# Modulation of a two-layer trunk: split fp32r products in two blocks, or plain fp32 products spread between the stages, with the loads of x on another queue

## The reference, cut to what matters

```python
def ada_params(cond, w_mod, b_mod):
    m = jax.nn.silu(cond) @ w_mod + b_mod          # w_mod: 1024 x 6144, one per layer
    return jnp.split(m, 6, axis=-1)

for layer in range(2):
    mp, ms = ada_params(c_ctx, ...), ada_params(c, ...)
    h = rms_norm(x, norm1) * (1 + m[1]) + m[0]
    x = x + m[2] * mixer(h)                        # layer 0: even mixer (scan), layer 1: attention and convolution
    h = rms_norm(x, norm2) * (1 + m[4]) + m[3]
    x = x + m[5] * ff(h)                           # layer 0: dense SwiGLU, layer 1: mixture of 8 experts
```

## Time and profile before

| what | value |
|---|---|
| median of 3 runs | 2351.88 us (2350.11 to 2356.47) |
| the profiled execution | 2351.2 us, span 2349.6 us |
| PE, DVE, ACT, POOL busy | 84%, 54%, 36%, 14% |
| modulation of layer 0, PE | 31.0 to 105.2 us, with the turning of x in it |
| modulation of layer 1, PE | 867.3 to 933.8 us |
| last remainder of norm 0, of norm 2 | 153.0 us, 985.4 us |

### The profile page before, as it was taken

The page is one execution under the profiler, slowest core; times in us unless marked ns, Lnnn a source line. Parts: engine busy times, 40 slices in busy tenths (PEclk is TensorE's granted clock), DMA queues, the critical chain, the costliest instruction groups (busy, mean ns, idle before and its releaser), DMA issues.

```text
span 2349.6 us, 35825 instructions
## 1 busy us (share of the span) xinstructions
PE 1967.4 (84%) x12234; PEld 1730.1 (74%) x12235; DVE 1257.9 (54%) x2029; ACT 856.9 (36%) x1348; POOL 327.8 (14%) x350
## 2 busy tenths in 40 slices
PE   4789486999999996898878886697978888896985
PEld 2489285999999983795333574697967888896983
DVE  4733764223323347315987547244866777865435
ACT  4722712222122237222223322243644655553321
POOL 2030202000000000205960003002101011101011
PEclk9979787999999999698577897798989998998996
DMA  9902011324621249222000021246867699866433
GB/s 286 313 21 73 18 37 45 108 78 128 161 80 42 74 143 329 76 72 54 3 0 0 1 78 63 65 119 184 231 178 213 181 254 260 237 191 169 122 90 134
DMA packets 439521, 288.47 MB, mean 123 GB/s; under 512 B 20890, under 2 KB 428666, under 8 KB 439332
## 3 DMA queue, kind: packets, MB, share of 16 engines
q1 hardware_dynamic: 425124, 248.75, 36.6%
q0 software_dynamic: 13024, 37.12, 5.3%
q10 hardware_dynamic: 1184, 0.51, 0.1%
HBM read 262.86 MB, written 23.47 MB: 122 GB/s over the span
## 4 chain that ended last, share of the span: by engine, by line
PE 67%; DVE 15%; issue 9%; ACT 3%; SPq 2%; DMA 2%; POOL 1%; ACTq 1%; DVEq 0%; POOLq 0%
PE ps L983 14%; PE ps L984 14%; PE ps L985 14%; PE ps L988 11%; PE ps L989 4%; DVE vp L1824 2%; PE ps L1051 2%; SPq L464 2%; DVE lo L1555 2%; PE ps L1269 1%; PE ps L1286 1%; ACT hi L613 1%; POOL tmp L2208 1%; DVE am L1885 1%; DVE h_both L1646 1%
## 5 line engine op out<-in xcount | busy, mean ns | idle before, releaser
L1555 DVE TENSOR_TENSOR lo<-raw,hi 128x1024 fp32r<-128x1024 f32 (+3 forms) x538 | 566.6, 1081 | 200.6 <-ACT hi L613 195.7
L613 ACT ACTIVATE hi<-raw 128x1024 fp32r<-128x1024 f32 (+3 forms) x538 | 495.6, 942 | 403.5 <-PE ps L985 255.9
L983 PE MATMUL ps<-h_both,hi 128*128 128x320 f32 x1728 | 546.8, 316 | 62.4 <-DVE h_both L1646 30.4
L984 PE MATMUL ps<-h_both,hi 128*128 128x320 f32 x1728 | 541.7, 313 | 0.0
L985 PE MATMUL ps<-h_both,lo 128*128 128x320 f32 x1728 | 541.6, 313 | 0.0
L983 PEld LDWEIGHTS ps<-h_both,hi 128*128 128x128 f32 x1728 | 330.8, 191 | 72.7 <-issue 41.0
L988 PE MATMUL ps<-h_both,hi 128*128 128x256 f32 (+2 forms) x1056 | 295.6, 367 | 60.8 <-issue 52.0
L984 PEld LDWEIGHTS ps<-h_both,hi 128*128 128x128 f32 x1728 | 331.6, 192 | 0.2 <-issue 0.2
L985 PEld LDWEIGHTS ps<-h_both,lo 128*128 128x128 f32 x1728 | 331.2, 192 | 0.0
L988 PEld LDWEIGHTS ps<-h_both,hi 128*128 128x128 f32 x1056 | 211.7, 200 | 70.3 <-issue 53.2
L989 PE MATMUL ps<-h_both,lo 128*128 128x128 f32 (+2 forms) x1056 | 257.6, 244 | 0.0
(11 more groups left out here) (324 smaller groups left out, 2617.3 us busy)
## 6 DMA issues: line engine op xcount, KB each, us to landing
raw<-in_moe_w_dram SPq DMA_DIRECT2D x160, 512.0 KB, 5.2
raw<-in_w_mod_dram SPq DMA_DIRECT2D x96, 512.0 KB, 7.7
raw<-in_moe_w_dram SPq DMA_DIRECT2D x64, 384.0 KB, 3.5
raw<-in_ff_w_dram SPq DMA_DIRECT2D x40, 512.0 KB, 4.9
raw<-in_moe_w_dram SPq DMA_DIRECT2D x64, 320.0 KB, 3.8
y_rows<-zeros POOLq DMA_DIRECT2D x22, 512.0 KB, 4.2
raw<-in_moe_w_dram SPq DMA_DIRECT2D x32, 256.0 KB, 2.9
raw<-in_ev_w_in_dram SPq DMA_DIRECT2D x12, 512.0 KB, 8.8
```

The source lines that it names most:

```text
L613: act.activation(hi[c % 2][:, parts[h]], raw[c % 4][:, parts[h]], ACT.Copy).then_inc(hi_done, 1)
L983: pe.matmul(out, w_hi, v_hi, start=first, stop=False, skip_group_check=True)
L984: pe.matmul(out, w_hi, v_lo, start=False, stop=False, skip_group_check=True)
L1555: dve.tensor_tensor(lo[c % 2][:, parts[h]], raw[c % 4][:, parts[h]], hi[c % 2][:, parts[h]].bitcast(F32), ALU.subtract).then_inc(lo_done, 1)
```

## The change

The products of the modulation are made without a split. The stationary operand is `cs`, two columns of plain fp32, and the 256 moving columns come straight from the `raw` buffer, in plain fp32: 8 matmuls a chunk, and no `hi`, no `lo`. PE itself releases the buffer (`mod_done`). ACT copies the result to one of two short rows (`mod_row`), PE turns it at once with two transposes of 2 rows (`fold`), and where a group of chunks ends ACT copies the group out of PSUM (`mod_keep`) and DVE adds the bias (`mod_params`).

The 48 chunks no longer stand in two blocks. They come as 8 ahead of `EIN` (around the turning of x and around norm 0), 12 in the mixer, 8 behind the sums of norm 1, 8 around norm 2, 8 ahead of attention, 4 behind the sums of norm 3. The ring of buffers counts them in that order, so loads of the other weights move with them. `split` of the two chunks of the next projection now stands inside norm 0 and behind norm 3; it stood in the modulation's loop and behind `OOUT`. PE waits for `mod_kept` ahead of `EIN`, `EOUT`, `FF`, `OIN` (twice), the first product with v in attention, and the turning behind the router.

The loads of x are begun on ACT's queue right behind `mats`, ahead of the 21 loads of parameter rows; POOL's queue loses them and the load of `sel4`. The loops over the two `FF` items are written out on SP, ACT and DVE. The gates use six banks instead of eight and the swap one bank instead of two, so that the modulation has banks of its own.

```diff
+MODS = [(0, 8, 0), (8, 12, EOUT + 2), (20, 8, FF + 2), (28, 8, OIN + 2), (36, 8, OOUT + 2), (44, 4, MOE)]
+KEPT = [(0, 8), (8, 12), (20, 4), (24, 4), (28, 4), (32, 4), (36, 8), (44, 4)]
...
             act.dma_start(mats[:, :, :], a["const_mats"].rearrange("m p c -> p m c")).then_inc(mats_in, 16)
+            for t in range(TT):
+                src = a["x_prompt"][0] if t == 0 else a["x_sample"][0, (t - 1) * P:t * P, :]
+                act.dma_start(xrows[:, t, :], src).then_inc(x_in, 16)
             act.wait_ge(prow_zero, 1)
...
+            def mod_row(first, count=1):
+                for q in range(first, first + count):
+                    act.wait_ge(mod_done, q + 1)
+                    if q >= 2:
+                        act.wait_ge(mod_folded, q - 1)
+                    act.activation(mrow[:, q % 2, :], ps[0:2, mod_bank(q), 0:256], ACT.Copy).then_inc(mod_rows, 1)
...
-            mod_fours(0, X_AFTER)
+            mod_row(0, 4)
...
-            mod_fours(X_AFTER, N_MOD // 4)
+            mod_row(4, 2)
...
+                if first is not None:
+                    first()
                 for k in range(KT):
                     act.wait_ge(n_aff, KT * i + k + 1)
                     act.activation(hh[:, k, :], tmp[:, k % 2, 0:T] if h is None else h[:, k, :], ACT.Copy).then_inc(n_hi, 1)
+                    if with_k is not None and k % 2:
+                        with_k(k // 2)
...
+            def first_weights():
+                mod_row(6, 2)
+                mod_keep(0)
+                split_hi(EIN)
+                split_hi(EIN + 1)
...
+            norm_act(1, lambda k: (evac, 2 * (EOUT + k // 2 + 1)), first=lambda: mod_row(20), with_k=lambda c: mod_row(21 + c))
...
-            act.wait_ge(evac, 2 * M1)
-            mod_fours(0, N_MOD // 4 - 1, M1, mrow1)
...
+            norm_act(2, lambda k: (evac, 2 * OIN), first=rest_of_first, with_k=lambda c: mod_row(32 + c))
...
+            def mod_chunk(q):
+
+                r = ring_of_mod(q)
+                w = raw[r % 4][:, :].rearrange("p (k c) -> p k c", k=KT)
                 for k in range(KT):
...
+                    if k % (KT // 2) == 0:
+                        pe.wait_ge(slot_in[r % 4][k // (KT // 2)], 16 * landed(r))
+                    if k == 0 and q >= 2:
+                        pe.wait_ge(mod_rows, q if mod_bank(q) == 7 else q - 1)
+                    last = pe.matmul(ps[0:2, mod_bank(q), 0:256], cs[:, k, :], w[:, k, :], start=k == 0, stop=k == KT - 1, skip_group_check=True)
+                last.then_inc(mod_done, 1)
...
-            norm_pe(0)
-            fold(mrow)
+            mods(4, 2)
+            norm_pe(0)
+            mods(6, 2, True)
+            pe.wait_ge(mod_kept, 1)
...
+            mods(20, 8, True)
+            pe.wait_ge(mod_kept, 4)
...
-            with pe.Fori(0, N_MOD // 2) as pr:
-                for u in range(2):
-                    begin(M1 + 2 * pr + u)
-                    mod_chunk(u, M1 + 2 * pr + u)
+            mods(28, 2)
             pe.wait_ge(evac, 2 * OIN)
             norm_pe(2)
-            fold(mrow1)
+            mods(30, 2, True)
+            pe.wait_ge(mod_kept, 5)
+            mods(32, 4, True)
+            pe.wait_ge(mod_kept, 6)
```

More of the change, by code:

```diff
@@ L49, with ring_of, ring_of_mod, landed @@
 N_ITEM = N_UP + KT
[L50 to L57, removed]
+EIN, EOUT, FF, OIN, OOUT, MOE = 0, 6, 10, 50, 57, 61
+MODS = [(0, 8, 0), (8, 12, EOUT + 2), (20, 8, FF + 2), (28, 8, OIN + 2), (36, 8, OOUT + 2), (44, 4, MOE)]
+KEPT = [(0, 8), (8, 12), (20, 4), (24, 4), (28, 4), (32, 4), (36, 8), (44, 4)]
+X_BANKS = (4, 6, 7)
+def ring_of(n):
+    return n + sum(count for _, count, before in MODS if before <= n)
+def ring_of_mod(q):
+    return q + [before for first, _, before in MODS if first <= q][-1]
+MANY = [(ring_of(OIN + c), 3) for c in range(2)] + [(ring_of(OOUT + c), 1) for c in range(4)]
+def landed(r):
+    return r // 4 + 1 + sum(more for m, more in MANY if m <= r and m % 4 == r % 4)
+def taken_before(r):
+    for q in range(2 * N_MOD):
+        if ring_of_mod(q) == r - 4:
+            return "mod", q
+    for n in range(MOE):
+        if ring_of(n) == r - 4:
+            return "weight", n
 JH = 6
@@ L525, in _ @@
-            sp.dma_start(hsel[:, :, :], a["const_hsel"]).then_inc(odd_in, 16)
-            sp.dma_start(hspread[:, :, :], a["const_hspread"]).then_inc(odd_in, 16)
+                return up_proj, up_part, down_proj
+            mods(0)
+            for c in range(6):
+                load(EIN + c, columns(a["ev_w_in"][0], c * 256))
+            for c in range(2):
+                load(EOUT + c, columns(a["ev_w_out"][0], c * 256))
+            mods(1)
+            for c in range(2, 4):
+                load(EOUT + c, columns(a["ev_w_out"][0], c * 256))
@@ L626, in mod_fours @@
-            def mod_fours(start, end, first=M0, mrow=mrow):
-                with act.Fori(start, end) as pr:
-                    for u in range(4):
-                        mod_evac(u % 2, first + 4 * pr + u, 4 * pr + u, mrow)
-                        split_hi(first + u + 2, pr, fine=True)
-            mod_fours(0, X_AFTER)
+            act.activation(cs[:, :, 0], par[:, 1, CX:CX + KT], ACT.Silu)
+            act.activation(cs[:, :, 1], par[:, 1, CS:CS + KT], ACT.Silu).then_inc(cs_silu, 1)
+            act.wait_ge(ab_lam, 1)
@@ L993, in begin @@
                 pe.wait_ge(lo_done, 2 * n + 1)
[L994 removed]
+                if not isinstance(n, int) or n >= 2:
+                    pe.wait_ge(evac, 2 * (n - 1) if free is None else free)
             def second(n):
@@ L1641, in norm_dve @@
                 t_of(1)
+                if first is not None:
+                    first()
                 for k in range(KT):
-                    if k == 3 and layer is not None:
-                        mod_params(layer, 1)
                     dve.wait_ge(n_hi, KT * i + k + 1)
@@ L1648, in norm_dve, with first_weights @@
                         t_of(k + 2)
-            norm_dve(0, layer=0)
+            def first_weights():
+                mod_params(0, part=0)
+                split_lo(EIN)
+                split_lo(EIN + 1)
+            norm_dve(0, first=first_weights)
             for c in range(2):
```

382 lines of the change are left out of this document (205 added, 177 removed).

## The result

| | before | changed |
|---|---|---|
| median of the runs | 2350.99 us (4 runs, 2347.61 to 2356.47) | 2261.07 us (4 runs, 2253.32 to 2263.03) |
| profiled execution, its span | 2351.2 us, 2349.6 us | 2261.82 us, 2260.2 us |
| granted clock, mean | 0.892 | 0.926 |

The ratio is 0.9609, 95% interval 0.958 to 0.9639.

The account below looks back on a forecast made before the run. PE, busy 84% of the span, was taken to wait in stretches, among them both modulation blocks (DMA full, DVE nearly). Terms -48 + 6 + 10 - 67 + 16 + 6 = -77 on 2351.2 us gave 2274 us, range 2246 to 2312.

Parts of the forecast that it names:

- The price of a chunk: All 48 chunks on PE: 16 records, 3.55 us each at full clock, 3.9 with the two transposes.
- The first rival: Spread chunks don't raise the clock, 7.0 us each: 2320 in part (chance 0.15), 2440 throughout (0.03), no change (0.01).
- The start: Up to the last remainder of norm 0: at 104.9 us instead of 152.99, 48 us less.
- The second rival: At the start, parameter rows get nothing until x is through and land 13.5 us later, at 40: 2286 us; chance 0.12.
- The mixer: Mixer and `EOUT`: 12 chunks, 47 us, into 41 us of idle PE, clock gain gives back 3: 6 us more.
- Norm 1: From the sums to the feed-forward part's first products: eight chunks come first, 412.4 against 402.5, 10 us more.
- row 24 is copied behind k = 7, then chunks 26 and 27: End of norm 1: 402.7 + 0.4 + 3.9 + 3.9 + 1.5 = 412.4 us on the old time axis.
- Norm 2 and `OIN`: From the end of `FF`: 118 us to the last remainder before, now a sum of 51: 67 us less.
- ahead of attention: Between `OIN` and attention: five chunks at 1.5 us, two at 7.8 less 4, then 4: 16 us more.
- The third rival: Mixer and attention take their chunks for nothing, clock gains pay: 2252 us; chance of better than 2255: 0.13.
- Router: Four chunks behind the sums of norm 3, gated by norm copies; 1.5 less for splits before squares: 6 us more.
- Behind the router: From the end of the router's product to the end of the kernel: no difference, 0.

Follow-up runs that it names:

- the two blocks: Changed kernel with its plain fp32 chunks put back in two blocks of 24, ahead of `EIN` and behind the feed-forward part: 2364.08 us, ratio 1.0044.
- the kernel with standing weights: Changed kernel with the roles in a chunk's product exchanged: fp32 weights stand, two columns of silu(c) move, no row copies or transposes back: 2354.9 us, ratio 1.0043.

## Why the prediction was right

**The price of a chunk** came from the sums of norm 1, scaled by columns: 3.55 us, measured 3.6. With the fold 3.76 instead of 3.9, since the two transposes of 2 columns need 0.15 to 0.2 us in the sequence, not the 0.35 of two full ones. 48 x 0.14 is 7 us of PE's time, of which some 30% lie on the path: 2 us, spread over the stages below.

**The clock.** The first rival (low clock) needed records 0.43 us apart. They are 0.216 apart from 35.6 us on, but for two chunks: number 37 ahead of attention took 5.30 us behind a wait of 2.69 us, and number 46 ahead of the router 5.15 us behind one of 3.89. At the start the clock rose 5.6 us behind the first chunk, where I had taken 5. In norm 1 and the mixer the granted clock is 1.00.

**The start**, -48 against -48.5. The rows were due at 28.2 and came at 28.1, but the reason that I gave for it is only half of what happens. I had x begun at 11 us, as on GpSimd's queue. On ScalarE's it is begun from 1.47 us on, which pushes the issue of the last row from about 13 to 18.9 us; and that row lands 9.0 us after its issue instead of 13.5. The changed kernel's chain of waits has:

```profile
18.93 9.04 DMA prow<-in_k_norm_dram
```

5.8 later and 4.4 quicker is the 1.4 us measured. That the two nearly cancel to the forecast's 1.6 is luck. The second rival (rows that wait for x, 2286 us) put 13.5 us on the rows, from a landing of x that began at 11 us among the modulation's weights; begun at 1.47, x had landed at 22.8 us, and the last row at 28.0. The Trainium skill's "DMA: Bandwidth & Descriptors", section "Queues, rings and completion order", which stands behind it (a ring's descriptors are taken in order), isn't contradicted: the last row did land behind x, but x needed only 3.9 us more when that row was issued. The kernel with x on GpSimd's queue puts the price of being behind x at 2.0 us.

**The mixer**, +6 against +3.1. The mixer itself grew by 6.3 us, as forecast, though the clock rose in the whole stage (0.73 to 1.00). What I had not counted is `EOUT`: from its first product to the one from which it runs without a gap it took 7.75 us instead of 10.33, and 0.6 less from there on.

**Norm 1**, +10 against +12.9. The step "row 24 is copied behind k = 7, then chunks 26 and 27" is met: 9.8 us forecast from that copy's end to the first product, 358.69 to 368.51 measured. What was missing is clock, twice. The sums took 10.24 us instead of 8.85, at a granted clock of 0.86; and the feed-forward part took 466.4 us from its first product where five other kernels with spread chunks need 464.9. Neither is shown to be an effect of the change: in the kernel before with only the loads of x moved, these sums took 11.8 us. And I had taken the late row for a part of the design's cost, when it was a place in a queue: rows 22 to 24 were each 1.23 us late, and one line undoes it.

**Norm 2 and `OIN`**, -67 against -69.2, and **ahead of attention**, +16 against +17.1: the steps are found in the trace. `OIN`'s first product comes 44.3 us behind the end of the feed-forward part and its full stream 50.5, forecast 51. The terms that I gave ahead of attention (7.5, 3.8 and 4) add up to 15.3, not 16. The third rival (mixer and attention for nothing, 2252) was wrong ahead of attention: the clock gives back 2.2 of the 3.76 us of a chunk in a round.

**Router**: +7.5 against +7.8. The 1.5 us for the squares that no longer stand behind splits were 3.0, and the sums gained 1.6 by a better clock, 10.35 to 8.77 us: 3 us more than forecast. The 1.6 are not shown to come from the change either: with only the loads of x moved the old sums took 8.85 us.

**Behind the router** the forecast had 0 and the traces differ by 6.7 us. Nothing there has changed. The windows view of that stretch in the changed kernel:

```profile
1347.20:2259.90 912.70, 759.85 (x5293) 723.62 (x5293) 553.10 (x1014) 392.52 (x603) 101.69 (x165) 0.91 0.61 176
```

and in the kernel with standing weights, the same instructions:

```profile
1442.10:2349.50 907.40, 761.38 (x5293) 724.43 (x5293) 554.71 (x1016) 392.02 (x605) 101.22 (x165) 0.90 0.62 179
```

It took 919.4 us before and in the two blocks, and 913.1 to 916.6 in the six others that compute the same. So over all profiled executions it moves by 12 us, and the two of the old form (919.4 and 916.6) lie among those of the new one: the 6.7 us are no effect of the change that these runs can show. Of the 12 us between forecast and profile half are here; the other half is the sum of small terms, 3 in the mixer, 3 at the sums and squares of norm 3, 1 in attention, 2 in norm 2, less 3 in norm 1 and 1 ahead of attention. It is the same spread that hides a 2 us edit in the times while the milestones show it.

## What to carry to other kernels

Work that needs only PE and loads, and is needed late, is cheapest in the idle stretches of stages that other engines bound: here 48 chunks of 3.76 us put some 50 of their 180 us on the path (an estimate: six of eight products were worth 38 us up to the router, so all eight some 51), though as a block they cost more than the version that they replace. When work is spread in this way, look at the smallest helper that each piece needs from another engine (here a 0.37 us copy): queued one place too late behind copies that wait for something else, it cost some 17 us over three norms. And price a wait on PE with the half clock that can follow it: 1.7 us in `OIN` behind the wait of 4.45.

## What was not expected of the hardware

- Products of 128x128 fp32 blocks with 2 moving columns cost the same at full clock as 256 moving columns against 2 standing ones (0.112 us x 32 and 0.22 us x 16), but in norm 1 the granted clock fell from 1.00 to 0.50 after some 4 us of them, although PE was busy throughout; with the moving weights it was 1.00 in the same stretch.
- With six of eight products left out PE was busy for 14.6 of 32.3 us in norm 1, at a granted clock of 0.61 against 1.00, so the sparing of work gave back less than its time.
- The granted clock is shown as 1.00 at the start of an execution, where the distance between records (0.427 against 0.216 us) says it is half.
- The part of the program behind the router, unchanged, took between 907 and 919 us in ten profiled executions.
